# Latent attention scores: the rotated part times the keys' low part as two 64-row products in different row halves

## What is computed

```python
q = (_rmsnorm(q_a, q_a_norm_g) @ w_q_b).reshape(b, s, MLA_HEADS, MLA_NOPE + MLA_ROPE)   # 128 + 64
q_nope = q[..., :MLA_NOPE]
q_pe = _rope(q[..., MLA_NOPE:], positions)
k_pe = _rope(k_pe[:, :, None, :], positions)[:, :, 0]                # one for all heads
sc = (jnp.einsum('bqhd,bkhd->bhqk', qn, k_nope, preferred_element_type=f32)
      + jnp.einsum('bqhr,bkr->bhqk', qp, k_pe, preferred_element_type=f32)) * scale
p = jax.nn.softmax(sc, axis=-1)
return jnp.einsum('bhqk,bkhd->bqhd', p.astype(v.dtype), v)
```

## Time and profile before

| | |
|---|---|
| median of three executions | 2965.27 us (2963.93 to 2967.96) |
| profiled execution | 2960.16 us, span 2958.4 us |
| mean granted clock of PE | 0.97 |
| busy in the span | PE 2756.4 us (93%), PE weight loads 2190.7, DVE 1688.1, ACT 1332.5 |
| latent attention | about 1060 to 1530 us of the span |
| line 1982, the products that the change replaces | 128 products of 512 columns |

### The profile page before, as it was taken

The page is one execution under the profiler, slowest core; times in us unless marked ns, Lnnn a source line. Parts: engine busy times, 40 slices in busy tenths (PEclk is TensorE's granted clock), DMA queues, the critical chain, the costliest instruction groups (busy, mean ns, idle before and its releaser), DMA issues.

```text
span 2958.4 us, 35313 instructions
## 1 busy us (share of the span) xinstructions
PE 2756.4 (93%) x13229; PEld 2190.7 (74%) x13229; DVE 1688.1 (57%) x2247; ACT 1332.5 (45%) x1906; POOL 0.2 (0%) x4
## 2 busy tenths in 40 slices
PE   6999999996799989999998899988899999999998
PEld 4777777774677767877876667666677878878787
DVE  7678888887676534444455635554664424434345
ACT  5666676663323234444443435655334323223233
POOL 0000000000000000000000000000000000000000
PEclk9999999997899989999999899999799999999999
DMA  7311111101445400000022210000211111111112
GB/s 256 105 36 50 44 35 50 50 28 56 164 135 168 128 16 10 16 6 9 6 100 98 75 37 22 22 15 15 100 36 50 45 48 48 45 50 41 52 37 87
DMA packets 218307, 176.75 MB, mean 60 GB/s; under 512 B 9610, under 2 KB 203106, under 8 KB 218210
## 3 DMA queue, kind: packets, MB, share of 16 engines
q1 hardware_dynamic: 216688, 171.07, 18.4%
q10 hardware_dynamic: 1522, 4.37, 0.4%
HBM read 158.12 MB, written 17.30 MB: 59 GB/s over the span
## 4 chain that ended last, share of the span: by engine, by line
PE 79%; DVE 8%; ACT 6%; DVEq 2%; DMA 2%; issue 2%; SPq 1%; ACTq 0%
PE PS L510 18%; PE PS L512 18%; PE PS L511 18%; PE PS L1296 4%; PE PS L1999 4%; PE PS L1269 2%; PE PS L1283 2%; PE PS L1273 1%; PE PS L1989 1%; PE PS L2490 1%; PE PS L2503 1%; PE PS L1960 1%; DMA gated<-in_w_ada 1%; PE PS L2514 1%; DMA activations<-in_ada_w 1%
## 5 line engine op out<-in xcount | busy, mean ns | idle before, releaser
L510 PE MATMUL PS<-h_high,w_high 128*128 128x512 f32 x2096 | 842.9, 402 | 47.7 <-DVE w_low L532 18.4
L511 PE MATMUL PS<-h_low,w_high 128*128 128x512 f32 x2096 | 824.6, 393 | 0.0
L512 PE MATMUL PS<-h_high,w_low 128*128 128x512 f32 x2096 | 824.2, 393 | 0.0
L510 PEld LDWEIGHTS PS<-h_high,w_high 128*128 128x128 f32 x2096 | 398.8, 190 | 147.2 <-issue 43.8
L512 PEld LDWEIGHTS PS<-h_high,w_low 128*128 128x128 f32 x2096 | 398.2, 190 | 85.5
L511 PEld LDWEIGHTS PS<-h_low,w_high 128*128 128x128 f32 x2096 | 398.7, 190 | 80.1 <-issue 1.7
L532 DVE TENSOR_TENSOR w_low<-raw_weights,w_high 128x1024 fp32r<-128x1024 f32 (+2 forms) x156 | 179.5, 1153 | 159.1 <-ACT w_high L527 158.2
L527 ACT ACTIVATE w_high<-raw_weights 128x1024 fp32r<-128x1024 f32 (+2 forms) x156 | 155.9, 1000 | 234.5 <-PE PS L512 232.0
L1373 ACT ACTIVATE residual<-PS,rest 128x1024 f32<-128x1024 f32 x128 | 141.5, 1111 | 179.0 <-DVE rest L1503 179.0
L3065 DVE SCALAR_TENSOR_TENSOR gated<-rest,gated 128x1024 f32<-128x1024 f32 x44 | 56.6, 1286 | 253.2 <-ACT gated L3033 253.2
L850 DVE SCALAR_TENSOR_TENSOR residual<-PS,rest,residual 128x512 f32 (+1 forms) x104 | 76.2, 749 | 153.5 <-PE PS L512 149.0
(11 more groups left out here) (359 smaller groups left out, 4165.2 us busy)
## 6 DMA issues: line engine op xcount, KB each, us to landing
raw_weights<-in_w_in SPq DMA_DIRECT2D x59, 512.0 KB, 4.2
raw_weights<-in_w_up SPq DMA_DIRECT2D x44, 512.0 KB, 3.8
gated<-in_w_ada SPq DMA_DIRECT2D x12, 1536.0 KB, 7.1
raw_weights<-in_w_out SPq DMA_DIRECT2D x24, 512.0 KB, 3.7
residual<-x_kept SPq DMA_DIRECT2D x3, 4096.0 KB, 13.9
rest<-in_ada_w SPq DMA_DIRECT2D x16, 576.0 KB, 4.9
activations<-in_ada_w SPq DMA_DIRECT2D x8, 1024.0 KB, 14.1
x_kept<-residual SPq DMA_DIRECT2D x2, 4096.0 KB, 13.2
```

The lines of the kernel that those rows point to most:

```text
L510: e.matmul(out_, wh[:, k, :], xh[:, k, cols], start=first, stop=False)
L511: e.matmul(out_, wh[:, k, :], xl[:, k, cols], start=False, stop=False)
L512: return e.matmul(out_, wl[:, k, :], xh[:, k, cols], start=False, stop=last_k)
```

## The change

The high part of the rotated queries is kept a second time, in the other row half of a tile of its own, QPD, which lies in XT's free slice 7. The four products of a half's rotated part become: QPS x KPP as before for both halves of the keys, and then, behind all eight full products, one product of 64 rows for each half of the keys: the high part of the queries from QPS in the own rows for keys 0 to 511, the same from QPD in the other rows for keys 512 to 1023, each against KPLL's copy of the keys' low part in those rows. The product of the two low parts is no longer made. For this ACT makes a second copy of 64 x 1024 in `act_rope`, and signals behind both. Since QPD lies in XT, x comes back in two pieces: slices 0 to 6 as before, slice 7 when all 64 score groups are through; DVE waits for both (48 in place of 32, and 80 in place of 64 later on).

```diff
--- before.py
+++ after.py
@@ -621,7 +621,12 @@
         e.wait_ge(s["x_kept"], (16, 32, 64)[turn])
         for sm, v in free:
             e.wait_ge(sm, v)
-        e.dma_start(XT[:, :, :], x_kept.rearrange("t p n -> p t n")).then_inc(s["x_back"], 16)
+        if turn == 1:
+            e.dma_start(XT[:, 0:7, :], x_kept[0:7].rearrange("t p n -> p t n")).then_inc(s["x_back"], 16)
+            e.wait_ge(*latent["scored"])
+            e.dma_start(XT[:, 7, :], x_kept[7]).then_inc(s["x_back"], 16)
+        else:
+            e.dma_start(XT[:, :, :], x_kept.rearrange("t p n -> p t n")).then_inc(s["x_back"], 16)
         if turn == 2:
             e.dma_start(RR, r_kept).then_inc(s["x_back"], 16)
 
@@ -1859,6 +1864,7 @@
             (QNH, QNL, KNH, KNL)[n][i] = rounded(f"{NAMES[n]}{i}", R.at(S), S)
         QPS = [rounded(f"q_rope_high_low{i}", (li_sq_at, li_sqq_at)[i], S) for i in range(2)]
         QPE = view(li_sqc_at, S)
+        QPD = rounded("q_rope_high_other", xt_at + 7 * S, S)
         E = [R(S), R(S)]
         PT = R(NT, 2 * P)
         V = R(NT, P)
@@ -1979,7 +1985,11 @@
                 e.matmul(out_, QNH[p][:, qs_], KNL[p][:, ns], start=False, stop=False)
                 e.matmul(out_, QNL[p][:, qs_], KNH[p][:, ns], start=False, stop=False)
                 e.matmul(out_, QPS[p][:, qs_], KPP[:, ns], start=False, stop=False)
-                last = e.matmul(out_, QPS[p][:, qs_], KPLL[:, ns], start=False, stop=True)
+            for n in range(2):
+
+                rows = slice(64 * (n ^ p), 64 * (n ^ p) + 64)
+                last = e.matmul(banks(2 * (q % 2) + n), (QPS[p], QPD)[n][rows, qs_], KPLL[rows, n * HALF:(n + 1) * HALF],
+                                start=False, stop=True)
             last.then_inc(sc, 1)
 
         def pe_trans(e, t, q):
@@ -2066,9 +2076,10 @@
 
         def act_rope(e, t, odd, after):
 
-            own = slice(64 * odd, 64 * odd + 64)
+            own, other = slice(64 * odd, 64 * odd + 64), slice(64 - 64 * odd, 128 - 64 * odd)
             e.wait_ge(low, after)
-            e.activation(QPS[odd][own, :], QPE[own, :], ACT.Copy).then_inc(qs, 1)
+            e.activation(QPS[odd][own, :], QPE[own, :], ACT.Copy)
+            e.activation(QPD[other, :], QPE[own, :], ACT.Copy).then_inc(qs, 1)
 
         def act_exp(e, t, q):
             e.wait_ge(mx, 8 * t.h + (q + 1))
@@ -2223,7 +2234,7 @@
             for k in range(5, 7):
                 early_parts[0].g_low(e, k)
 
-        return dict(sync=sync, tensor=tensor, scalar=scalar, vector=vector, pj=(pj, 56), gated=(gt, 17))
+        return dict(sync=sync, tensor=tensor, scalar=scalar, vector=vector, pj=(pj, 56), gated=(gt, 17), scored=(sc, 64))
 
     A_W = 256
     B_AT, C_AT, QKV = 2 * A_W, 2 * A_W + 3 * 384, 384
@@ -3195,7 +3206,7 @@
     latent_in = latent_input([out0.slot_done(0), None], norm1)
     early_out1 = []
     latent = latent_attention(latent_in, early_out1)
-    out1 = OutProj("w_out1", 0, NT, 24 + 16, True, [latent["pj"]], [latent["pj"]], [latent["gated"]], 32, H2, 3,
+    out1 = OutProj("w_out1", 0, NT, 24 + 16, True, [latent["pj"]], [latent["pj"]], [latent["gated"]], 48, H2, 3,
                    final="final_norm_g")
     out1.high_done = 7
     early_out1.append(out1)
@@ -3207,7 +3218,7 @@
     early_parts = []
     windows = dilated_windows(stick, gating, early_parts)
     out2 = OutProj("w_out_2", 0, NT, 64, True, [], [(mp_pj, 36)],
-                   [windows["fin"]], 64, H2, 5, rescale=True)
+                   [windows["fin"]], 80, H2, 5, rescale=True)
     out2.slot_free = [(mp_pj, 32), (mp_pj, 34)]
     early_parts.append(out2)
     norm4 = NormHalves(out2, 0, lambda t: gains[:, 8 + t:9 + t], shift_col(72))
```

## The result

The changed kernel takes 2973.45 us (median of 13 runs, 2969.21 to 2979.27), the kernel before in the same sessions 2964.13 (13 runs): a ratio of 1.0031, 95% interval 1.0023 to 1.0040, or +9.3 us (+6.8 to +11.9). The change makes the kernel slower by 0.31%, which is more than the 0.2% that can be told from nothing.

A forecast was written before the change was run, and what follows sets the result against it. PE was taken as nearly the bound, busy 106 of 112 us in heads 2 and 3. Pair +2.6, copies +5.0 and fetch 0 make +7.6 us on the median 2965.3: 2972.9 us, spread 2969 to 2977.

The forecast's parts named there:

- The copies: ACT's second copy of rotated queries delays DVE's subtraction 1.0 us in four even heads and before the first: +5.0 us.
- The pair: Two 64-row products ending each score group cost more than the full products they replace: +2.6 us over the stage.
- The steps in and out: On PE at a score group's end: 0.32 us from the last full product to the pair, 0.43 to a following product.
- block 4's transposes: In the four even heads, block 4's 0.10 us lies in a wait the late copies make: 2.9 us, not 3.3.
- head 7: Last head, PE waiting in nearly every block: only the pair's earlier last result counts, some -0.3 us.
- Rival A: A lone pair costs what one product does: 11.1 us gained, less 5.0 for copies, 2959.2 us; chance 0.10.
- six groups a head: Of eight score groups PE issues in a head, six lie on the chain, each 0.23 us shorter if a pair costs one product.
- Rival B: Copies hidden in the loop or pair neutral, one term gone or halved: +2.6 to +5.5, about 2969 us; chance 0.27.
- the 0.42 us wait of PE for DVE: PE's wait at 1216.52, before block 3's transposes in head 2, taken as evidence against the copies being hidden.
- Rival C: Everything pays: 8 copies at 1.0 and 56 groups at 0.15 us, 16.4 us more, 2981.7 us; chance 0.06.
- The fetch: Fetching x in two pieces on SP's queue costs 0, with 20 us of cover; without cover, 3.7 us once.

## Why the prediction was right, and where it was off

**Direction and sum.** I said +7.6 us and 2972.9; it is +9.3 and 2973.45. The forecast held by both of its terms, each of which has now been run alone; both came out somewhat above what I had set, so the total is not near by two errors that cancel. Heads 2 and 3 were to take about 114 us together; they took 115.6, and 114.0 without head 3's slower stretch.

**The copies: +5.0, measured +5.6, and right in its places.** Alone they cost 1.06 us in head 2, nothing in head 3, and before the first head 1.07. Four even heads and the start make 4 x 1.06 + 1.07 = 5.3. I had set 1.0 a place because ACT's next instruction starts a little before the last one's recorded end; the second copy does not, it starts 1.07 after the first (1213.98, 1215.05). That the price in the even heads is DVE's late start, and that cover decides it, is shown by two kernels that each take it away there without taking the copy away.

**The pair: +2.6; alone +4.1 (1.5 to 6.8), and 3.0 by the heads.** The steps in and out were right to the hundredth (0.32 and 0.43); the product behind has 0.34 to its successor, where 0.23 + 0.09 would be 0.32. (The prediction says that all 64 groups of the first layer enter at 0.32. By the trace 59 do; in five the clock was at the lower level and it took 0.49 to 0.56.) What was mis-sized is the sum over the heads. I set 0.47 us a head and took 0.10 off in the even ones, because block 4's transposes would hide behind the late copies. Heads without a slower stretch show 0.41 to 0.48, in even and odd heads alike, in the changed kernel, with the signal first and without the copy: nothing is hidden there. In head 2 of the changed kernel the pair and the copy make 1.06 + 0.41 = 1.47, their plain sum. So seven heads make about 3.1 and not 2.9, and head 7, for which I had set -0.3, gave -0.1: together 3.0. That the cost lies in blocks 4 to 7 is shown by the kernel with the pair in these alone. Sum of the two terms by the profile: 5.3 + 3.0 = 8.3.

**What is left, about 1 us,** lies inside the interval, and the clock can move more than that either way. The profiled changed kernel had a slower stretch in head 3 and one in head 5, 1.5 us each, where the kernel before had none; in head 1 it was the other way round, and the kernel before had one more in the steps ahead of head 0's first product with the values. From the first copy to the last product with the values, all stretches included, the profiles give 452.4 us before and 460.5 us changed, +8.1. The same count for the copies alone is 454.5, only +2.1, because that kernel had neither the stretch in head 1 nor the one ahead of head 0. So a sum of steady parts can't be read off one pair of profiles as a whole, and that it comes within 1 us of the whole runs is in part luck. Each stretch stands in one profile of one execution; that the change causes them isn't shown.

**Rival A, the pair at the price of one product, -11.1 + 5.0.** Excluded as to the price of the pair. Its sum was wrong besides: I had counted six groups a head as being on the way. One product less in each group is -6.5 us in all and 1.09 us, 4.7 groups, in head 2. The step that failed is the count of the groups on the chain. It took each group at its full 0.23 us, where PE's next wait eats up a part of it: the chain shows what was last, not by how much. With this A would have come to -6.5 + 5.3, about -1 us, and not to a faster kernel that can be told from the old one. The chance of 0.10 for faster was too much for that reason too.

**Rival B** had 0.27 for a hidden copy or a neutral pair. Neither was (+5.6 and +4.1 alone, both intervals above 0); the 0.42 us wait of PE for DVE in the earlier trace rows was indeed the sign that no cover was left. **Rival C,** +16.4, is excluded: the interval ends at 11.9, and head 3 with the copies alone pays nothing.

**The fetch: 0, right.** The second piece has some 24 us of cover (issued 1520.03, landed 3.4 later, first needed 1547.05). The copies-only kernel includes it and leaves nothing over that its interval shows.

No version with the pair beats the kernel before. The best of those that compute the scores as the change does, the signal after the first copy, is still 3.6 us slower (0.9 to 6.2), since the pair itself costs more than the product that it saves.

## What to carry to other kernels

Going from 128-row to 64-row work and back cost 0.3 to 0.4 us here, more than the 0.23 us of a 512-column product that a lone pair of half-height products saves. Several pairs in a row might pay: an estimate from the earlier trace rows, where a second pair starts 0.33 us behind the first, is 0.32 + 0.33 + 0.33 + 0.10 = 1.08 us for two pairs with the way in and out, against 1.16 for five steps of full products. No run here tries it. Before counting PE time as gained, leave the instruction out and measure; of 1.9 us less per head 1.1 arrived, in a loop in which PE was busy 95% of the time (105.97 of 112.00 us). And when a second write is put behind a first one, signal each to those who wait for it: one line moved took back the 1.06 us a head that the even heads had paid.

## What I had not expected of the hardware

The steps at the change between 128 and 64 rows came out the same with two pairs in a row (first layer), with one pair, and with two products in one half: at a clock of 1.00 it took 0.32 us from a 512-column product into them, and out again 0.10 to 0.11 over the step of a product and another 0.10 at the next one. With the pair at the group's start, leaving took the same 0.43 and 0.33.

The second thing is the granted clock. From head 2 on the profiled attention had no stretch at the lower level in the kernel before and with the copies alone, the early signal, the pair without the copy, the order alone or the copies behind step 3; it had one with the pair first, with the pair in four blocks and with one product less, and two with the changed kernel, the 64-row products in one half and two products less. A single one costs 1.5 us (head 3 of the changed kernel). These came with less work on PE as well as with more. Head 1 shows another pattern: all six kernels without the second copies had one there (before, pair without the copy, 64 rows in one half, order alone, one and two products less), all six with them had none. From head 1 on all fell in odd heads. With one profile of each kernel I can name no rule and no cause. By these profiles the stretches are a part of why two products less gave only 9.2 us, and they limit how finely such kernels can be compared by whole runs.
